# A two-layer encoder trunk on one core: first gather split, softmax by head parity, weight parts requested in another place

## What is computed

```python
h = h + conformer_conv_module(h, ...)          # layer 0
h = h + hierarchical_moe(h, ...)
k, v = shared_mla_kv(h, ...)
h = h + mla_attention_layer(h, k, v, ...)      # layer 1
h = h + hierarchical_moe(h, ...)

# hierarchical_moe, over all 32 experts
a, b = jnp.split(xt @ w_gu, 2, axis=-1)
acc + ((jax.nn.silu(a) * b) @ w_d) * g[:, None]
```

## Time and profile before

| | |
|---|---|
| median of 3 runs | 1118.01 us (1117.9 to 1118.22) |
| the profiled execution | 1118.59 us, its span 1116.9 us |
| TensorE busy | 1008.0 us, 90% of the span |
| VectorE, ScalarE, GpSimd busy | 238.0, 173.5, 58.4 us |
| moved by DMA | 430.73 MB, mean 386 GB/s |
| chain that ended last | TensorE 48%, DMA 40%, VectorE 7%, SyncE's queue 4%, ScalarE 1% |

### The profile page before, as it was taken

How to read it: one execution, slowest core, us unless ns; L and a number is a source line. 1 busy time by engine, 2 the same in 40 slices (tenths; PEclk the granted TensorE clock), 3 DMA queues, 4 the chain that set the end, 5 groups by cost and what they waited for, 6 DMA issues and landing times.

```text
span 1116.9 us, 11486 instructions
## 1 busy us (share of the span) xinstructions
PE 1008.0 (90%) x4848; PEld 435.5 (39%) x4848; DVE 238.0 (21%) x525; ACT 173.5 (16%) x438; POOL 58.4 (5%) x92
## 2 busy tenths in 40 slices
PE   8999999989897989889799899999998979897887
PEld 7885532333232323223265554332323232232322
DVE  5993411201020100101035714201010101020101
ACT  4865300000000000000045513000000000000000
POOL 2890000000000000000000000000000000000000
PEclk9999999999999999999999999999999999999999
DMA  9794899999999999999996558999999999999997
GB/s 313 215 365 165 344 428 428 429 427 428 427 429 427 427 430 427 426 428 429 395 383 222 226 209 328 430 428 428 425 430 428 425 431 425 428 429 425 431 421 287
DMA packets 61073, 430.73 MB, mean 386 GB/s; under 512 B 12264, under 2 KB 22591, under 8 KB 38238
## 3 DMA queue, kind: packets, MB, share of 16 engines
q1 hardware_dynamic: 60894, 429.86, 93.8%
q10 hardware_dynamic: 126, 0.14, 0.0%
HBM read 428.94 MB, written 1.05 MB: 385 GB/s over the span
## 4 chain that ended last, share of the span: by engine, by line
PE 48%; DMA 40%; DVE 7%; SPq 4%; ACT 1%; issue 1%; DVEq 0%
DMA ring<-in_w_down_dram 25%; PE bank L941 15%; DMA zone<-in_w_down_dram 14%; PE bank L988 11%; PE bank L1026 6%; DVE bank L1324 4%; PE bank L930 3%; PE bank L1220 2%; PE bank L879 2%; SPq L446 2%; PE bank L1113 1%; PE bank L1135 1%; PE bank L1089 1%; PE bank L1097 1%; DMA pos_i<-in_positions_dram 1%; PE bank L997 1%
## 5 line engine op out<-in xcount | busy, mean ns | idle before, releaser
L941 PE MATMUL bank<-ring,zone 128*32 128x512 f32 x1152 | 337.0, 612 | 39.2 <-DMA ring<-in_w_gate_up_dram 26.8
L941 PE MATMUL bank<-zone 128*32 128x512 f32 x872 | 276.4, 608 | 25.6 <-DMA zone<-in_w_gate_up_dram 13.9
L988 PE MATMUL bank<-ring,xT 128*32 128x512 f32 x592 | 161.8, 593 | 13.0 <-DMA ring<-in_w_down_dram 6.8
L941 PEld LDWEIGHTS bank<-ring,zone 128*32 128x32 f32 x1152 | 87.8, 113 | 219.2 <-issue 218.9
L941 PEld LDWEIGHTS bank<-zone 128*32 128x32 f32 x872 | 70.7, 112 | 145.7 <-issue 145.4
L1447 DVE TENSOR_TENSOR xT<-xT,bank 128x512 f32<-128x512 f32 x16 | 11.0, 687 | 459.6 <-PE bank L941 459.6
L988 PE MATMUL bank<-zone,xT 128*32 128x512 f32 x304 | 103.9, 593 | 4.9 <-DMA ring<-in_w_down_dram 2.0
L1452 DVE TENSOR_TENSOR h<-bank,h 128x512 f32<-128x512 f32 x64 | 44.2, 691 | 266.6 <-PE bank L1026 266.6
L682 ACT ACTIVATE xT<-bank 128x512 f32<-128x512 f32 x16 | 9.6, 597 | 539.5 <-PE bank L941 539.5
L988 PEld LDWEIGHTS bank<-ring,xT 128*32 128x32 f32 x592 | 42.2, 110 | 94.8 <-issue 88.5
L1026 PE MATMUL bank<-zone,xT 128*128 128x512 f32 x128 | 63.1, 615 | 1.8 <-ACT zone L692 1.6
(11 more groups left out here) (264 smaller groups left out, 649.8 us busy)
## 6 DMA issues: line engine op xcount, KB each, us to landing
ring<-in_w_gate_up_dram SPq DMA_DIRECT2D x72, 2048.0 KB, 35.1
zone<-in_w_gate_up_dram SPq DMA_DIRECT2D x54, 2048.0 KB, 33.6
ring<-in_w_down_dram SPq DMA_DIRECT2D x40, 2048.0 KB, 35.7
zone<-in_w_down_dram SPq DMA_DIRECT2D x20, 2048.0 KB, 37.0
ring<-in_a_pw_w_dram SPq DMA_DIRECT2D x8, 1024.0 KB, 12.2
ring<-in_w_down_dram SPq DMA_DIRECT2D x8, 1024.0 KB, 17.7
ring<-in_a_pw_w_dram SPq DMA_DIRECT2D x2, 2048.0 KB, 11.4
ring<-in_w_o_dram SPq DMA_DIRECT2D x2, 2048.0 KB, 21.0
```

What stands on the lines that cost most here:

```text
L941: ins = nc.tensor.matmul(bank[b][s * CAP:(s + 1) * CAP, :], xs[:, k, s * CAP:(s + 1) * CAP], rhs[s][:, b * HALF:(b + 1) * HALF], start=(k ...
L988: ins = nc.tensor.matmul(bank[2 + b][s * CAP:(s + 1) * CAP, :], hidT[:, k, s * CAP:(s + 1) * CAP], units[s][:, k, b * HALF:(b + 1) * HALF] ...
```

## The change

It does nine things.

- **First gather split.** `gather` can do a part of the k. Before the first quad it does k = 0 to 4 (10 products); k = 5 to 7 (6 products) come behind the products of unit 0.
- **Two parts of the unit apart early.** Parts 2 and 3 are requested ahead of the waits for `pw2_done` in layer 0 (behind unit 6), and ahead of the wait for `logits_done` in layer 1 (behind unit 9). For that the router's weights of layer 0, `wr[0]`, move out of `spare` to `zone`, and their transfer waits until the convolution's weights are transposed (`cols_tr`, 2).
- **Softmax of tile 0 by head parity.** Even heads first: mask, largest, exponents, division, transposes, values and `w_o` go by four even and four odd heads, with VectorE's order rewritten. `oT` and `pT0` are copied by parity.
- **A wait before the second half of `w_o` of tile 0**, for `smax_ready` 3, since bank 7 holds scores until then.
- **Table load.** A square root of one element (`warm`) is put behind ScalarE's exponents of tile 1, in front of its wait for the second `o_done`.
- **Block 3 of the input** is copied to `xT` by VectorE in place of ScalarE.
- **Short filler**: 6 products in place of 14 at the start.
- **Last quad**: the scatter of tile 1 of the first half moves behind the last products of down.
- All later counts of `xT_ready` rise by one.

```diff
-        wr = [spare[:, SP0:SP0 + KD * NR].rearrange("p (k r) -> p k r", r=NR), sb("wr1", [P, KD, NR])]
-        SP1 = SP0 + KD * NR
+        wr1 = sb("wr1", [P, KD, NR])
+        SP1 = SP0
...
+        wr = [zone[:, moe0:moe0 + KD * NR].rearrange("p (k r) -> p k r", r=NR), wr1]
...
+        EVEN_ODD = (0, 2, 4, 6, 1, 3, 5, 7)
...
-                return pT0[:, 4 * n:4 * n + 4, :]
+                return by_parity(pT0)[:, n, :, :]
...
+            sp.wait_ge(cols_tr, 2)
             for l in range(L):
...
+            def parts_apart(l, parts):
+
+                for s in parts:
+                    src = a["w_gate_up"][l][s, 0:HALF, :].rearrange("(p k) c -> p k c", k=4)[:, APART, :]
+                    sp.dma_start(unit_apart[s], src).then_inc(apart_in, 16)
+
             def experts(l, first):
                 e = E[l]
                 for g in AHEAD + [g for g in range(SLOTS, EARLY) if g != SLOTS + APART]:
                     if g == APART:
+                        if l == 1:
+                            parts_apart(1, (2, 3))
                         sp.wait_ge(logits_done, 2 * l + 2)
-                        for s in range(SIDE):
-                            src = a["w_gate_up"][l][s, 0:HALF, :].rearrange("(p k) c -> p k c", k=4)[:, APART, :]
-                            sp.dma_start(unit_apart[s], src).then_inc(apart_in, 16)
+                        parts_apart(l, (0, 1))
...
                 if g == 7:
+                    sp.wait_ge(hb_ready, 2)
+                    parts_apart(0, (2, 3))
                     sp.wait_ge(pw2_done, 3)
...
-            for b in (1, 3):
-                t = b // 2
-                act.wait_ge(tr_done, b + 1)
-                for j in range(4):
-                    ins = nc.scalar.activation(xT[:, 4 + j, t * P:(t + 1) * P], bank[b][:, j * P:(j + 1) * P], ACT.Copy,
-                                               scale=col("a_norm_g", 4 + j))
-                ins.then_inc(xT_act, 1)
+            act.wait_ge(tr_done, 2)
+            for j in range(4):
+                ins = nc.scalar.activation(xT[:, 4 + j, 0:P], bank[1][:, j * P:(j + 1) * P], ACT.Copy, scale=col("a_norm_g", 4 + j))
...
-                act.wait_ge(smax_ready, t + 1)
-                for hh in range(H):
+                for i, hh in enumerate(EVEN_ODD):
+                    if t == 0 and i % 4 == 0:
+                        act.wait_ge(smax_ready, i // 4 + 1)
+                    if t == 1 and i == 0:
+                        act.wait_ge(smax_ready, 3)
...
+                if t == 1:
+                    nc.scalar.activation(warm[:, :], eps_c[:, :], ACT.Sqrt)
                 act.wait_ge(o_done, 2 * t + 2)
-                nc.scalar.copy(oT[:, 4:8, t * P:(t + 1) * P], bank[1][:, :].rearrange("p (h q) -> p h q", h=4)).then_inc(o_act, 1)
+                nc.scalar.copy(by_parity(oT)[:, 1, :, t * P:(t + 1) * P], bank[1][:, :].rearrange("p (h q) -> p h q", h=4)).then_inc(o_act, 1)
...
-            for _ in range(14):
+            for _ in range(6):
...
-                def gather(n):
+                def gather(n, part=range(KD)):
 
                     pe.wait_ge(e["pick_ready"], n + 1)
-                    for k in range(KD):
+                    for k in part:
...
+                                if k == 0:
+                                    gather(n, range(5, KD))
...
-                    scatter(n, 0)
+                    scatter(n, 0, tiles=(0,))
                     down_rows(KF - 1, 1, landed(UNITS - 1)).then_inc(e["used"], 1)
+                    scatter(n, 0, tiles=(1,))
                     scatter(n, 1)
...
-                    for t in range(TT):
+                    for t in tiles:
...
-                gather(0)
+                gather(0, range(0, 5))
...
-                pe.wait_ge(p_ready, t + 1)
                 for n in ((0, 1), (2, 3, 4, 5))[t]:
+                    pe.wait_ge(p_ready, min(n, 2) + 1)
                     for j in range(4):
-                        src = sc0[:, 4 * n + j, :] if n < 2 else sc1[:, 2 * (n - 2) + j // 2, (j % 2) * P:(j % 2 + 1) * P]
+                        src = sc0[:, 2 * j + n, :] if n < 2 else sc1[:, 2 * (n - 2) + j // 2, (j % 2) * P:(j % 2 + 1) * P]
                         ins = nc.tensor.transpose(bank[prob_bank(n)][:, j * P:(j + 1) * P], src, ident[:, :])
...
-                pe.wait_ge(pT_act, 1 + 2 * t)
-                for hh in range(H):
+                if t == 1:
+                    pe.wait_ge(pT_act, 3)
+                for hh in EVEN_ODD:
+                    if t == 0 and hh == 1:
+                        pe.wait_ge(pT_act, 1)
                     for kt in range(t + 1):
-                        ins = nc.tensor.matmul(bank[hh // 4][:, (hh % 4) * P:(hh % 4 + 1) * P], v_tok[:, kt, hh, :],
+                        ins = nc.tensor.matmul(bank[hh % 2][:, (hh // 2) * P:(hh // 2 + 1) * P], v_tok[:, kt, hh, :],
                                                pT0[:, hh, :] if t == 0 else pT1[:, hh, kt, :],
                                                start=(kt == 0), stop=(kt == t))
-                    if hh % 4 == 3:
+                    if hh >= H - 2:
                         ins.then_inc(o_done, 1)
...
-                pe.wait_ge(o_act, t + 1)
                 for hf in range(2):
-                    for hh in range(H):
+                    if t == 0 and hf == 1:
+                        pe.wait_ge(smax_ready, 3)
+                    for hh in EVEN_ODD:
+                        if hf == 0 and hh == 1:
+                            pe.wait_ge(o_act, t + 1)
                         ins = nc.tensor.matmul(bank[wo_bank(2 * t + hf)][:, :], oT[:, hh, t * P:(t + 1) * P],
...
-            for b in (0, 2):
+            for b in (0, 2, 3):
...
-            def minus_max(t):
-                link(V.tensor_reduce(smax[:, t, :], sc0 if t == 0 else sc1, AX_X, ALU.max))
-                V.tensor_scalar(smax[:, t, :], smax[:, t, :], -1.0, None, ALU.mult).then_inc(smax_ready, 1)
-
-            def probs(t):
-
-                dve.wait_ge(exp_done, (t + 1) * H)
-                link(V.reciprocal(sinv[:, t, :], ssum[:, t, :]))
-                sc = sc0 if t == 0 else sc1
-                V.tensor_tensor(sc, sc, over(sinv[:, t, :], (t + 1) * P), ALU.mult).then_inc(p_ready, 1)
+            def minus_max(top, of):
+                link(V.tensor_reduce(top, of, AX_X, ALU.max))
+                V.tensor_scalar(top, top, -1.0, None, ALU.mult).then_inc(smax_ready, 1)
+
+            def probs(total, one_over, p, w, exps):
+
+                dve.wait_ge(exp_done, exps)
+                link(V.reciprocal(one_over, total))
+                V.tensor_tensor(p, p, over(one_over, w), ALU.mult).then_inc(p_ready, 1)
+
+            def max_of_half(w):
+                minus_max(head_parity(smax[:, 0, :])[:, w, :], by_parity(sc0)[:, w, :, :])
+
+            def probs_of_half(w):
+                probs(head_parity(ssum[:, 0, :])[:, w, :], head_parity(sinv[:, 0, :])[:, w, :], by_parity(sc0)[:, w, :, :], P, 4 * w + 4)
...
-            masked(0)
+            link(masked(0))
+            max_of_half(0)
             link(masked(1))
-            minus_max(0)
-            for n in range(2, 5):
-                masked(n)
-            probs(0)
+            max_of_half(1)
+            masked(2)
+            probs_of_half(0)
+            masked(3)
+            probs_of_half(1)
+            probs_across(0)
+            masked(4)
+            heads_out(0)
             link(masked(5))
-            probs_across(0)
-            minus_max(1)
-            heads_out(0)
-            probs(1)
+            minus_max(smax[:, 1, :], sc1)
+            probs(ssum[:, 1, :], sinv[:, 1, :], sc1, S, 2 * H)
             add_attention(0)
```

27 lines of the change are left out of this document (16 added, 11 removed).

## The result

The changed kernel takes 1111.63 us in the median of 5 executions (1111.29 to 1112.91), the kernel before 1118.01 beside it: a ratio of 0.9941, 95% interval 0.993 to 0.9953. The forecast was 1112.0. The profiled execution after is the one of 1111.29, its span 1109.6.

What follows compares the result with a forecast made beforehand. DMA at 425 to 431 GB/s was taken to bound the experts, engines the thin stretches; 1118.59 - 1.3 - 1.3 - 2.7 - 0.4 - 0.9 - 0.1 + 0.4 = 1112.3, adjusted towards the median to 1112.0 us, range 1110.4 to 1115.0.

Steps and rivals of the forecast that it cites:

- First gather: Gather ahead of the first quad in each layer: splitting it frees the first place earlier, -1.3 us per layer.
- The rival that the change doesn't restart the stream earlier: TensorE's pace in quads 0 and 1 sets when DMA is full; split gather gives nothing: 1114.6 us, chance 0.07.
- Parts 2 and 3 early: 1 MB a layer requested before the gather only lengthens the dry stretch: 0; bounds -1.0 and +0.4 us each.
- Softmax: Attention, tile 0 by even and odd heads: `w_o` begins earlier, -2.7 us; bounds -3.3 and -1.0.
- The rival of TensorE's order: TensorE's in-order work swallows the split softmax; only 1.0 of 2.7 us won: 1113.7 us, chance 0.1.
- Table load: ScalarE's load before layer 1's router moves into its wait for tile 1's values: -0.4 us; bounds 0 and -0.5.
- Last quad: Last products of down come sooner: -0.9 us in layer 1, 0 if TensorE awaits the last megabyte; -0.1 in layer 0.
- Start: Kernel start with six fillers: part of the projection at the lower clock, +0.4 us; bounds 0 and +2.8.
- Low clock at the start: Projection's first block does half its work at 1.2 GHz: +2.8 us in place of +0.4, 1114.4 us, chance 0.2.
- Slower: Three blocks of the projection at the start run at 1.2 GHz: +21 us, 1132 us, chance 0.02.
- The waits in the experts: Inside the experts TensorE waits for DMA, with chain pieces such as 37.38 us of one transfer; engines worth nothing there.

## Why the prediction was right, and where not

The time was right to 0.4 us. By places in the two profiles, 1118.59 and 1111.29, the 7.3 us between them are: start 0.8, layer 0 from the router to its end 1.2, softmax 2.9, table 0.4, layer 1's gather 1.3, and from its first request to the end 0.8. The sum had +0.4, -1.4, -2.7, -0.4, -1.3 and -0.9. Behind places that agree the reasons did not always.

Beside the experiments the change won 7.2 to 7.4. Undone in turn, the gather with the parts (2.7), the softmax (2.6), the table load (0.5) and the scatter (0.2) come to 6.0. No run undid the copy of block 3 or the move of the router's weights, and the other 1.2 to 1.4 have no experiment; the start, 0.8 in the profiles, is among them.

- **First gather**, -1.3 a layer: right as a place in time (130.79), and right in layer 1. What it buys in layer 0 hangs on the hole in the stream. I read 168 GB/s in one stretch of the earlier trace rows as dry in layer 0. It holds little to win: with late parts the split brings layer 0's end forward by 0.27 in the profiles, and by nothing in the medians. The rival that the change doesn't restart the stream earlier was thus nearly true of layer 0 by itself, and fails because of the early parts.
- **Parts 2 and 3 early**, 0: the step that failed, though not in the sum. "This only lengthens the dry stretch" is true of the request as it stood before, not of one that comes 2 us earlier. Undone beside the split, they cost 1.9 to 2.2; with the gather whole, 0.3 at most. The two terms of layer 0 had to be costed as one: together they brought 1.2 in the profiles and 1.4 by the medians, where I had 1.3 + 0. That their sum came out is luck as far as the reasons go: I gave to the split alone what in layer 0 only the pair wins. One thing stays open: counted from the router's results, the 14-filler kernels with both edits undone and with the parts late end layer 0 after 439.9 and 439.8 us, the kernel before after 439.0, though it has late parts too. That the first of them is of the execution of 1114.9 may explain its 439.9. For the split with late parts the short filler shows 439.9 too, so it seems to be the longest of the four arrangements, and undoing the parts alone shows more (2.1) than the change brought (1.2). Why it would be longer than with both late is not shown.
- **Softmax**, -2.7: measured 2.88 in the trace, 2.6 in medians. My steps had the even transposes wait for tile 1's scores. They do, and by then the odd half is ready as well, so all eight go in one piece. The rival of TensorE's order found nothing.
- **Table load**, -0.4: 0.43 in the trace.
- **Last quad**, -0.9 in layer 1: 0.8 between the two profiles, 0.65 of it by this edit, at the low clock that both had there. The rows I drew it from, and the earlier trace rows, are of an execution whose clock had fallen behind the wait for the first tail piece, and I took them for every execution. With the clock held the edit is worth no more than 0.2: my lower bound, TensorE waiting for the last megabyte, is what happens. From the first request to the last addition, layer 1 takes 426.9 to 427.4 us in every experiment but the two with the finer gather. Layer 0, -0.1: nothing to see.
- **Start**, +0.4: it was -0.8. I looked at the projection; the end of the convolution hung on the positions. VectorE's last sum stands 67.0 us behind their arrival before, 67.2 after, and 67.0 to 67.4 in the ten experiments at full clock where they come near 15. They came at 15.74 before, at 14.80 after. How much of that is the change, and how much the moment at which the loads land, isn't separated: in the experiments they come at 14.77 to 15.30 whatever the filler. Requesting them ahead of the bias moved the end of the convolution by 1.17, but with the finer gather that run had, not the end of layer 0.
- **Low clock at the start**, the first rival with 0.2: it exists, in the profile with the whole gather, at 1.9 rather than 2.8 us. Its evidence against, the granted clock of 1.00 in the earlier trace rows, was weak for another reason than I gave: after the change the column says 1.00 from 7 to 11 us too, where the transposes take 3.68 us in place of 2.30. At the start the durations tell the level, not the column. The Trainium skill, "TensorE: Matmul & The Clock Gate", Part 4: PE-mode transpose, has transposes not count as busy in the way products do; the run with one filler speaks against that rule as I used it, since nothing else preceded a projection at full pace. The profile with the whole gather agrees with it in part: its clock fell while transposes ran (0.62 in the microsecond from 9).
- **Slower**, 21 us: nothing near it, even with one filler.
- **The waits in the experts**: I read the 37.38 us of the earlier trace rows as one transfer that TensorE waits for. They run from a request to its landing, behind others in the queue; from 224 to 261 us TensorE was busy for 32.8 of the 37. That the stream bounds the experts holds by the earlier trace rows.

## What to carry to other kernels

Where a stream of transfers runs dry, two edits on either side of the hole, bytes sent before it and a request made sooner behind it, are one edit: cost them together, and test them two by two. An earlier first request is worth no more than the gap that it fills, and is lost again if the second and third places come free no sooner. An idle time in front of the last work is no gain until the transfer behind it has been looked at, and the clock at which the rows of it were taken: here the same edit won 0.65 us at the low clock and 0.2 at the high one.

## What the hardware showed that I had not expected

- The granted clock can read 1.00 at the very start while every record takes the time of the lower level (16 transposes in 3.68 us against 2.30).
- The clock can fall again right after it rose, in some executions only: to 0.50 from 10 to 16 us, and in another kernel to 0.50 from 129 to 132 us, behind a wait in which TensorE was busy 0.26 and 0.46 of two stretches. There it cost the gather 0.7 us (1.85 for eight records, against 1.13 in the run whose clock held). At the end of layer 1, behind a wait of some 2.6 us, it fell in seven profiles (before, after, five experiments) and held in four; in three more the wait was 1.1 to 1.2 us, and it held.
- A queue refilled after it ran dry has a rough 2 us before it is at full rate: with the first place requested at 133.00 the engines moved 66 GB/s in that microsecond, then 180, 311 and 426.
